# A two-layer diffusion block and an MoE block on one core: the first projection starts with half of its tokens

## The chip, the cores and the metric
One core of one Trainium2 chip runs the whole computation in one launch. The metric is the device time in microseconds; the value of a kernel is the median of its runs. A separate profiled execution gives the trace.

## What is computed
A first block of two layers, then a second block, all in float32, on 256 latent tokens x and 256 context tokens ctx of width 1024. Only the start of the first layer matters here:

```python
silu_c, silu_cc = silu(c), silu(c_ctx)
shift, scale, gate       = split(silu_c  @ w_ada[0] + b_ada[0], 3)   # for the latents
shift_c, scale_c, gate_c = split(silu_cc @ w_ada[0] + b_ada[0], 3)   # for the context
u  = h  * (1.0 + scale)   + shift        # h  = x
uc = hc * (1.0 + scale_c) + shift_c      # hc = ctx
q, k, v, g     = split(u  @ a_w_in)      # 1024 -> 2560 columns
qc, kc, vc, gc = split(uc @ a_w_in)
```

Rotary embedding, windowed attention, an output projection and a normalisation follow, then a layer with neighbourhood attention, then the second block: attention beside a convolution, and a mixture of 32 experts.

## The kernel before, in words
**Tokens.** Activations are kept with features on the 128 partitions: tile j of `H` and `uT` holds features 128j to 128j+127 of all 512 tokens, columns 0 to 255 the latents, 256 to 511 the context. The inputs come token by token, so TensorE turns them: `turn_rows(half)` (L718) does two 128x128 transposes for each of eight tiles into PSUM banks 1 to 4 and waits from the fifth tile on for VectorE, which copies each tile of 256 columns into `H` (L1614 to L1617). Half 0 is x, half 1 ctx. `turn_taps` (L709) turns the convolution's weights for a much later stage.

**Weights.** Big weights are loaded in chunks of 1024x512 (2 MB) into a ring of six slots. `PLAN` (L111) fixes their order: ada0 column chunk 0, ada0 chunk 2, the first a_w_in chunk, ada0 chunks 1 and 3, the second a_w_in chunk, and so on. (This text counts ada0's chunks in the order of their use, from 0.) SyncE issues them in the loop at L553; x is issued after the first chunk and ctx after the second (L567), and from the seventh on SyncE waits until the slot's last reader on TensorE is done (L564). Each chunk has one semaphore count, `full[slot]`, on which `landed(n)` (L700) waits. The small vectors and the taps are issued by ScalarE at the start (L1324 to L1327).

**Modulation.** `stream("ada0", c, bank)` (L729) multiplies chunk c with the SiLU of the two conditioning vectors, in 64 small matmul instructions. ScalarE copies the row out of PSUM (L1340), `fold` (L747) turns it into columns, and VectorE's `take_half(half, bank)` (L1651) makes the scales and shifts of feature tiles 0 to 3 or 4 to 7: two additions and one more for 1 + scale. `modulate` (L1644) then makes `uT` tile by tile, x and ctx in turn, one step of `u_ok` per tile. Chunks 0 and 1 give what tiles 0 to 3 need, chunks 2 and 3 what tiles 4 to 7 need.

**First projection.** Its first chunk has four jobs of 128 output columns, one per PSUM bank. Each is the sum over eight feature tiles, and `half_job(i, ks)` (L835) does four of these with all 512 tokens. The order on TensorE is written out by hand: chunk 0, turn x, chunk 1, fold, turn ctx, turn taps, fold; wait for the taps and the chunk; lower halves of jobs 0 and 1, chunk 2, lower half of job 2, chunk 3, fold, lower half of job 3, fold; then the upper halves, each followed by a rotation for the rotary embedding (`beside`, L807). A float32 product counts as two instructions in the profile, a transpose as one. Behind that, `seven_products` (L858) does other chunks in seven products of half the size for eight.

Of the kernel before, what the change touches and what calls it, by code (L numbers as in the profile page):

```python
# [21 lines left out]
P = 128  # L22
D = 1024
KT = D // P
S = 256
# [202 lines left out]
def build(nc, IN, consts_dram, relpad, out):  # L228
    CA, CN = const_layout()
    with ExitStack() as ctx:  # L230
# [141 lines left out]
        cst_in, vec_in, sink_in = sem("cst_in"), sem("vec_in"), sem("sink_in")  # L372
# [4 lines left out]
        pe_x, x_ok = sem("pe_x"), sem("x_ok")  # L377
        sil_ok = sem("sil_ok")
# [157 lines left out]
        def _(sp):  # L536
# [16 lines left out]
            for n, (stage, src, l, c) in enumerate(PLAN):  # L553
                if n - SLOTS == PLACE["b_in"][5]:
                    sp.wait_ge(st["b_in"], used["b_in"][5])
                    load_bias(range(4))
                    sp.dma_start(late_tables, consts_dram[:, CA["dist"][0]:CA["mult"][1]]).then_inc(table_in, 16)
                if n == PLACE["ada1"][2]:
                    sp.wait_ge(tk["a_in", "dve"], len(DVE_ORDER["a_in"]))
                if n - SLOTS == PLACE["mod_a"][0]:  # L560
                    load_bias(range(4, NH))
                if n >= SLOTS:
                    was = PLAN[n - SLOTS][0]
                    sp.wait_ge(st[was], used[was][PLACE[was].index(n - SLOTS)])  # L564
                w = IN[src][l, :, c * COLS:(c + 1) * COLS].rearrange("(k p) n -> p k n", p=P)
                sp.dma_start(slot(n), w).then_inc(full[n % SLOTS], 16)
                if n in (0, 1):  # L567
                    rows = IN[("x", "ctx")[n]][0].rearrange("(t p) f -> p t f", p=P)
                    sp.dma_start(xrows[:, 2 * n:2 * n + 2, :], rows).then_inc(x_in[n], 16)
                if n == 5:  # L570
                    sp.dma_start(flat[:, 0:CN - CR], consts_dram[:, CR:CN]).then_inc(table_in, 16)
                    for c0, c1 in ((CF, CA["dist"][0]), (CA["mult"][1], CR)):
                        sp.dma_start(cst[:, c0:c1], consts_dram[:, c0:c1]).then_inc(table_in, 16)
# [123 lines left out]
        def _(pe):  # L697
# [11 lines left out]
            def turn_taps():  # L709

                pe.wait_ge(taps_in, 16)
                pe.wait_ge(vec_ok, 1)
                for c in range(4):
                    last = tr(ps[:, 0, 256 + 32 * c:256 + 32 * c + CONV_W], crows[:, c * P:(c + 1) * P],
                              ident[0:CONV_W, 0:CONV_W])
                last.then_inc(pe_vec, 1)

            def turn_rows(half):  # L718

                pe.wait_ge(x_in[half], 16)  # L720
                for j in range(KT):
                    i = half * KT + j
                    if i >= 4:
                        pe.wait_ge(x_ok, i - 3)
                    for t in range(2):
                        last = tr(ps[:, 1 + j % 4, t * P:(t + 1) * P], xrows[:, 2 * half + t, j * P:(j + 1) * P], ident)
                    last.then_inc(pe_x, 1)
# [37 lines left out]
            turn_rows(0)  # L765
            stream("ada0", 1, 6)
            fold("ada0", 0, 0, 2, 7)
            turn_rows(1)
            turn_taps()
            fold("ada0", 1, 0, 2, 7)  # L770
# [31 lines left out]
            def src_ready(stage, k):  # L802
                if stage == "a_in":
                    return u_ok, k + 1
# [30 lines left out]
            def half_job(i, ks):  # L835

                for k in ks:
                    if i == 0:
                        pe.wait_ge(u_ok, k + 1)
                    last = mm(ps[:, i, :], slot(PLACE["a_in"][0])[:, k, i * P:(i + 1) * P], uT[:, k, :],  # L840
                              start=(k == 0), stop=(k == KT - 1))
                if k == KT - 1:
                    last.then_inc(st["a_in"], 1)

            pe.wait_ge(taps_ok, 1)
            landed(PLACE["a_in"][0])
            half_job(0, range(4))
            half_job(1, range(4))
            stream("ada0", 2, 5)
            half_job(2, range(4))  # L850
            stream("ada0", 3, 6)
            fold("ada0", 2, 0, 2, 4)
            half_job(3, range(4))
            fold("ada0", 3, 0, 2, 4)
            for i in range(4):
                half_job(i, range(4, KT))
# [458 lines left out]
        def _(act):  # L1315
# [11 lines left out]
            act.dma_start(sink[:, :], IN["a_sink"].broadcast_to([P, NH])).then_inc(sink_in, 16)  # L1327
# [262 lines left out]
        def _(dve):  # L1590
# [23 lines left out]
            for i in range(2 * KT):  # L1614
                half, j = i // KT, i % KT
                dve.wait_ge(pe_x, i + 1)
                v.tensor_copy(H[:, j, half * S:(half + 1) * S], ps[:, 1 + j % 4, 0:S]).then_inc(x_ok, 1)  # L1617
            dve.wait_ge(pe_vec, 2)
            v.tensor_copy(conv_taps[:, :, :],
                          ps[:, 0, 256:384].rearrange("p (c k) -> p c k", c=4)[:, :, 0:CONV_W]).then_inc(taps_ok, 1)  # L1620
# [44 lines left out]
            dve.wait_ge(x_ok, 2 * KT)  # L1665
            settle()
            modulate(0, range(4))
            take_half(1, 4).then_inc(mod_ok, 1)
            dve.wait_ge(mod_ok, 1)
            modulate(0, range(4, KT))  # L1670
# [92 lines left out]
            dve.wait_ge(u_ok, KT)  # L1763
# [143 lines left out]
            dve.wait_ge(sink_in, 16)  # L1907
# [99 lines left out]
            dve.wait_ge(u_ok, 2 * KT)  # L2007
# [378 lines left out]
```

## Time and profile before

| what | us |
|---|---|
| median of 3 runs | 1213.71 |
| lowest and highest run | 1211.02, 1214.12 |
| the profiled execution | 1209.34 |
| its span in the trace | 1207.3 |
| TensorE busy (PE) | 1152.9 |
| VectorE busy (DVE) | 544.6 |
| ScalarE busy (ACT) | 295.7 |

The times of a trace are counted from the start of its span. The profiled execution's own time is 2.04 us longer than the span. PE is TensorE's matmuls, PEld its weight loads, which overlap them; SPq is SyncE's sequencer issuing transfers. An engine's idle time matters only where something on the way to the end waits for it. Matmuls are pipelined, so the duration of one is longer than its distance to the next.

### The profile page before, as it was taken

The page shows a single profiled execution, that of the slowest core. Times are in us where ns is not written, and L with a number is a line of the kernel's source. Part 1 is how long each engine was busy: PE and PEld are TensorE (multiplying, and loading weights), DVE is VectorE, ACT ScalarE, POOL GpSimd, SP SyncE. Part 2 cuts the span into 40 slices and gives each one's busy share as a digit, 9 for nine tenths or more (in the row PEclk, how much of TensorE's full clock was granted, in tenths as well). Part 3 has the DMA queues.
Part 4 walks back from the last instruction along what each step waited for, and adds up shares of the span by engine and source line. Part 5 has one row for each costly group of instructions (what it writes and reads, how often), then busy time and mean ns, then how long its engine had stood idle before and what let it go on. Part 6 is the DMA issues. An engine that isn't in the chain of part 4 may idle for free.

```text
span 1207.3 us, 17553 instructions
## 1 busy us (share of the span) xinstructions
PE 1152.9 (95%) x7148; PEld 743.0 (62%) x7148; DVE 544.6 (45%) x1278; ACT 295.7 (24%) x705; POOL 22.7 (2%) x33
## 2 busy tenths in 40 slices
PE   4999999989999999999998998999999999999996
PEld 3486876668778888668885585444444444444442
DVE  3353339986575430872799623122222222222223
ACT  0000128850340001660612413111111111111112
POOL 0000000000000001110000000000000000000000
PEclk9999999999999999999999798999999999999999
DMA  9852128023442226566376695999999999999990
GB/s 344 318 209 73 68 93 326 1 75 136 140 178 101 70 70 183 124 188 211 140 279 228 246 301 202 428 427 428 426 429 428 427 429 429 427 428 430 427 413 39
DMA packets 82335, 311.54 MB, mean 258 GB/s; under 512 B 18130, under 2 KB 19229, under 8 KB 69467
## 3 DMA queue, kind: packets, MB, share of 16 engines
q1 hardware_dynamic: 78672, 309.56, 65.9%
q10 hardware_dynamic: 3386, 0.86, 0.3%
q8 instruction: 48, 0.79, 0.3%
q0 software_dynamic: 208, 0.17, 0.1%
q14 instruction: 21, 0.16, 0.0%
HBM read 309.40 MB, written 1.18 MB: 257 GB/s over the span
## 4 chain that ended last, share of the span: by engine, by line
PE 81%; DVE 12%; ACT 2%; DMA 2%; issue 1%; SPq 1%; ACTq 0%; DVEq 0%
PE ps L1246 18%; PE ps L891 17%; PE ps L1278 9%; PE ps L1212 5%; PE ps L992 5%; PE ps L1224 5%; DVE G L2146 4%; PE ps L956 2%; PE ps L942 2%; PE ps L840 2%; PE ps L1096 2%; PE ps L1072 2%; PE ps L929 2%; PE ps L743 2%; DMA ring<-in_a_w_in 2%; DVE soft L1824 1%
## 5 line engine op out<-in xcount | busy, mean ns | idle before, releaser
L1246 PE MATMUL ps<-ring,prob 128*64 128x512 f32 x704 | 188.1, 593 | 1.2 <-issue 1.2
L1246 PEld LDWEIGHTS ps<-ring,prob 128*64 128x64 f32 x704 | 61.9, 137 | 100.3 <-issue 100.3
L2311 DVE TENSOR_TENSOR prob<-ps,prob 128x512 f32<-128x512 f32 x16 | 17.2, 1075 | 193.7 <-PE ps L1246 193.7
L1278 PE MATMUL ps<-ring,prob 128*64 128x512 f32 x352 | 78.0, 596 | 0.0
L891 PE MATMUL ps<-U,ring 128*128 128x256 f32 x304 | 69.9, 381 | 1.6 <-DVE Q L1991 1.3
L1246 PE MATMUL ps<-K,prob 128*64 128x512 f32 x160 | 70.3, 592 | 0.0
L1212 PEld LDWEIGHTS ps<-bias,U 128*128 128x128 f32 x512 | 60.5, 198 | 13.4 <-issue 13.4
L1387 ACT ACTIVATE prob<-ps,soft 128x512 f32<-128x512 f32 (+2 forms) x112 | 64.1, 591 | 11.0 <-DVE soft L1829 9.0
L2319 DVE TENSOR_TENSOR probT<-ps,cst 128x512 f32<-128x512 f32 x32 | 22.1, 691 | 94.6 <-PE ps L1278 94.6
L1212 PE MATMUL ps<-bias,U 128*128 128x128 f32 x512 | 63.5, 284 | 1.1 <-DVE bias L2272 1.1
L891 PEld LDWEIGHTS ps<-U,ring 128*128 128x128 f32 x304 | 57.6, 190 | 9.9 <-DVE Q L1991 1.7
L1224 PE MATMUL ps<-probT,bias 128*128 128x512 f32 x128 | 57.9, 594 | 0.0
L1551 ACT ACTIVATE prob<-ps 128x512 f32<-128x512 f32 x16 | 9.6, 597 | 192.4 <-PE ps L1246 192.4
L1404 ACT ACTIVATE probT<-ps 128x512 f32<-128x512 f32 (+1 forms) x88 | 48.2, 585 | 34.4 <-PE ps L942 33.6
L992 PE MATMUL ps<-U,ring 128*128 128x256 f32 x256 | 56.4, 381 | 0.0
L1544 ACT ACTIVATE prob<-ps,H 128x128 f32<-128x128 f32 x64 | 24.0, 456 | 128.3 <-PE ps L1212 128.3
L942 PE MATMUL ps<-cst,prob 128*128 128x128 f32 x344 | 51.6, 288 | 2.4 <-DVE prob L1850 2.4
L992 PEld LDWEIGHTS ps<-U,ring 128*128 128x128 f32 x256 | 48.4, 190 | 7.1 <-issue 0.8
L1278 PEld LDWEIGHTS ps<-ring,prob 128*64 128x64 f32 x352 | 24.3, 137 | 45.8 <-issue 45.8
L929 PE MATMUL ps<-K,Q 64*128 64x512 f32 (+1 forms) x192 | 46.9, 568 | 1.9 <-ACT G L1375 1.3
L2296 DVE TENSOR_TENSOR U<-ps,U 128x512 f32<-128x512 f32 x64 | 44.2, 691 | 8.9 <-PE ps L1224 8.9
L2146 DVE SCALAR_TENSOR_TENSOR G<-G,conv_taps 128x256 f32<-128x256 f32 x120 | 47.7, 478 | 0.0
(378 smaller groups left out, 1839.2 us busy)
## 6 DMA issues: line engine op xcount, KB each, us to landing
ring<-in_w_exp_gate SPq DMA_DIRECT2D x22, 2048.0 KB, 18.2
ring<-in_w_exp_up SPq DMA_DIRECT2D x20, 2048.0 KB, 16.7
ring<-in_w_exp_down SPq DMA_DIRECT2D x20, 2048.0 KB, 19.9
ring<-in_w_ada SPq DMA_DIRECT2D x12, 2048.0 KB, 16.4
ring<-in_w_mod SPq DMA_DIRECT2D x12, 2048.0 KB, 8.8
ring<-in_b_w_in SPq DMA_DIRECT2D x8, 2048.0 KB, 9.0
ring<-in_a_w_in SPq DMA_DIRECT2D x5, 2048.0 KB, 17.7
ring<-in_w_in SPq DMA_DIRECT2D x5, 2048.0 KB, 9.2
```

The source lines that it names most:

```text
L891: last = mm(ps[:, bank, 0:256], still[:, k, f * P:(f + 1) * P], moving[:, k, :], start=(k == 0), stop=(k == 3))
L929: last = mm(ps[:, 2 * (n % 2) + x, 0:len(kts) * P], q_of(h, kind, qb), k_of(h, kts), start=True, stop=True)
L942: last = tr(ps[:, 4 + i // 2, (i % 2) * S + x * P:(i % 2) * S + (x + 1) * P], prob[:, n % AHEAD, x * T + i * P:x * T + (i + 1) * P], ident)
L992: last = mm(ps[:, m % 4, 0:width], slot(n)[:, k, (m % 4) * P:(m % 4 + 1) * P], src[:, k, 0:width], start=(k == 0), stop=(k == KT - 1))
L1212: last = mm(ps[:, j // 4, (j % 4) * P:(j % 4 + 1) * P], h2rows[:, t, j * P:(j + 1) * P], pick[:, t, :], start=(t == 0), stop=(t == 1))
L1224: mm(ps[:, ACC_BANK[i], :], wpickT[:, t * P:(t + 1) * P], yrows[:, c * 512:(c + 1) * 512], start=True, stop=True).then_inc(scat, 1)
L1246: last = mm(ps[x * CAP:(x + 1) * CAP, 2 + i, :], xg[:, k, x * CAP:(x + 1) * CAP], chunk(n, 2 * i + x, turn)[0][:, k, :], start=(k == 0), s ...
L1278: last = mm(ps[x * CAP:(x + 1) * CAP, 5 + c, :], hidT[:, k, x * CAP:(x + 1) * CAP], chunk(n, 4 + x, turn)[0][:, k, c * 512:(c + 1) * 512], ...
L1387: last = a(prob[:, n % AHEAD, x * T:x * T + w], ps[:, 2 * (n % 2) + x, 0:w], ACT.Exp, bias=s[:, 1, x:x + 1], accum_out=None if L == "c" el ...
L1404: a(probT[:, i * S:i * S + w], ps[:, 4 + i // 2, 0:w], ACT.Copy).then_inc(at["copied"], 1)
L2146: ins = v.scalar_tensor_tensor(convo[:, j, :], glu[:, j, k:k + S], conv_taps[:, j, k:k + 1], convo[:, j, :], ALU.mult, ALU.add)
L2296: v.tensor_tensor(y, ps[:, b, :], y, ALU.add).then_inc(acc_ok, 1)
```

## The change
The loads: ada0's chunk 1 goes ahead of x; the first a_w_in chunk is split by feature tiles, the lower half (tiles 0 to 3) issued after x and ahead of ctx, the upper half after ada0's chunk 3. The lower half has a semaphore of its own, `lower_in`. The sink's load counts on the taps' semaphore, whose waits go to 32.

On TensorE: chunk 1 right behind chunk 0; four tiles of x turned into banks 1 to 4 of their own, both folds, the other four tiles in pairs (a pair fills a bank); the taps. Then the lower halves run on 256 columns at a time: jobs 0 and 1 on x, half of ctx turned, jobs 2 and 3 on x, the rest of ctx turned, and the same jobs on ctx with chunks 2 and 3 between them. The upper halves run on all 512 tokens, as before. VectorE copies pairs of tiles in one instruction (`take_rows`) and makes the first four tiles of u for x, then those for ctx. `u_ok` counts four more.

```diff
@@ -369,12 +369,13 @@
 
 
         table_in = sem("table_in")
-        cst_in, vec_in, sink_in = sem("cst_in"), sem("vec_in"), sem("sink_in")
+        cst_in, vec_in = sem("cst_in"), sem("vec_in")
         x_in, taps_in, taps_ok = [sem("x_in"), sem("ctx_in")], sem("taps_in"), sem("taps_ok")
         rel_in, rel_out, rel_zero = sem("rel_in"), sem("rel_out"), sem("rel_zero")
         full = [sem(f"full{i}") for i in range(SLOTS + 3)]
         pe_vec, vec_ok = sem("pe_vec"), sem("vec_ok")
         pe_x, x_ok = sem("pe_x"), sem("x_ok")
+        lower_in = sem("lower_in")
         sil_ok = sem("sil_ok")
         st = {n: sem(n + "_done") for n in ("ada0", "a_in", "a_out", "ada1", "b_in", "b_out", "mod_a", "c_in",
                                             "c_out", "mod_b")}
@@ -563,10 +564,17 @@
                     was = PLAN[n - SLOTS][0]
                     sp.wait_ge(st[was], used[was][PLACE[was].index(n - SLOTS)])
                 w = IN[src][l, :, c * COLS:(c + 1) * COLS].rearrange("(k p) n -> p k n", p=P)
-                sp.dma_start(slot(n), w).then_inc(full[n % SLOTS], 16)
-                if n in (0, 1):
-                    rows = IN[("x", "ctx")[n]][0].rearrange("(t p) f -> p t f", p=P)
-                    sp.dma_start(xrows[:, 2 * n:2 * n + 2, :], rows).then_inc(x_in[n], 16)
+                if n == PLACE["a_in"][0]:
+                    first_w = w
+                    sp.dma_start(slot(n)[:, 0:4, :], w[:, 0:4, :]).then_inc(lower_in, 16)
+                else:
+                    sp.dma_start(slot(n), w).then_inc(full[n % SLOTS], 16)
+                if n in (1, 2):
+                    rows = IN[("x", "ctx")[n - 1]][0].rearrange("(t p) f -> p t f", p=P)
+                    sp.dma_start(xrows[:, 2 * n - 2:2 * n, :], rows).then_inc(x_in[n - 1], 16)
+                if n == 4:
+                    first = PLACE["a_in"][0]
+                    sp.dma_start(slot(first)[:, 4:KT, :], first_w[:, 4:KT, :]).then_inc(full[first % SLOTS], 16)
                 if n == 5:
                     sp.dma_start(flat[:, 0:CN - CR], consts_dram[:, CR:CN]).then_inc(table_in, 16)
                     for c0, c1 in ((CF, CA["dist"][0]), (CA["mult"][1], CR)):
@@ -708,23 +716,20 @@
 
             def turn_taps():
 
-                pe.wait_ge(taps_in, 16)
-                pe.wait_ge(vec_ok, 1)
+                pe.wait_ge(taps_in, 32)
+                pe.wait_ge(x_ok, 4)
                 for c in range(4):
-                    last = tr(ps[:, 0, 256 + 32 * c:256 + 32 * c + CONV_W], crows[:, c * P:(c + 1) * P],
+                    last = tr(ps[:, 4, 256 + 32 * c:256 + 32 * c + CONV_W], crows[:, c * P:(c + 1) * P],
                               ident[0:CONV_W, 0:CONV_W])
                 last.then_inc(pe_vec, 1)
 
-            def turn_rows(half):
-
-                pe.wait_ge(x_in[half], 16)
-                for j in range(KT):
-                    i = half * KT + j
-                    if i >= 4:
-                        pe.wait_ge(x_ok, i - 3)
+            def turn_rows(half, js, bank):
+
+                for i, j in enumerate(js):
                     for t in range(2):
-                        last = tr(ps[:, 1 + j % 4, t * P:(t + 1) * P], xrows[:, 2 * half + t, j * P:(j + 1) * P], ident)
-                    last.then_inc(pe_x, 1)
+                        last = tr(ps[:, bank, i * S + t * P:i * S + (t + 1) * P],
+                                  xrows[:, 2 * half + t, j * P:(j + 1) * P], ident)
+                last.then_inc(pe_x, 1)
 
             def stream(stage, c, bank):
 
@@ -762,12 +767,15 @@
                 fold(stage, chunks[-1], v0, nv, to)
             pe.wait_ge(sil_ok, 1)
             stream("ada0", 0, 5)
-            turn_rows(0)
             stream("ada0", 1, 6)
+            pe.wait_ge(x_in[0], 16)
+            for j in range(4):
+                turn_rows(0, (j,), 1 + j)
             fold("ada0", 0, 0, 2, 7)
-            turn_rows(1)
+            fold("ada0", 1, 0, 2, 7)
+            turn_rows(0, (4, 5), 5)
+            turn_rows(0, (6, 7), 6)
             turn_taps()
-            fold("ada0", 1, 0, 2, 7)
 
             def in_proj(stage, src, widths, after=None, skip=0):
                 jobs = JOBS[stage]
@@ -801,7 +809,7 @@
 
             def src_ready(stage, k):
                 if stage == "a_in":
-                    return u_ok, k + 1
+                    return u_ok, 4 + k + 1
                 return nm["rms1", "out"], k + 1
 
             def beside(i):
@@ -832,28 +840,48 @@
                 mm(ps[:, 4 + n % 2, 0:S], rotm, src, start=True, stop=True).then_inc(rot_done, 1)
 
 
-            def half_job(i, ks):
-
-                for k in ks:
+            def lower_job(i, c0):
+
+                for k in range(4):
                     if i == 0:
-                        pe.wait_ge(u_ok, k + 1)
+                        pe.wait_ge(u_ok, (k + 1 if c0 == 0 else 4 + k + 1))
+                    mm(ps[:, i, c0:c0 + S], slot(PLACE["a_in"][0])[:, k, i * P:(i + 1) * P], uT[:, k, c0:c0 + S],
+                       start=(k == 0 and c0 == 0), stop=False)
+
+            def upper_job(i):
+
+                for k in range(4, KT):
+                    if i == 0:
+                        pe.wait_ge(u_ok, 4 + k + 1)
                     last = mm(ps[:, i, :], slot(PLACE["a_in"][0])[:, k, i * P:(i + 1) * P], uT[:, k, :],
-                              start=(k == 0), stop=(k == KT - 1))
-                if k == KT - 1:
-                    last.then_inc(st["a_in"], 1)
-
+                              start=False, stop=(k == KT - 1))
+                last.then_inc(st["a_in"], 1)
+
+            pe.wait_ge(lower_in, 16)
+            lower_job(0, 0)
+            lower_job(1, 0)
+            pe.wait_ge(x_in[1], 16)
+            turn_rows(1, (0, 1), 7)
             pe.wait_ge(taps_ok, 1)
+            turn_rows(1, (2, 3), 4)
+            lower_job(2, 0)
+            lower_job(3, 0)
+            pe.wait_ge(x_ok, 7)
+            turn_rows(1, (4, 5), 7)
+            pe.wait_ge(x_ok, 8)
+            turn_rows(1, (6, 7), 4)
+            lower_job(0, S)
+            stream("ada0", 2, 5)
+            lower_job(1, S)
+            stream("ada0", 3, 6)
+            lower_job(2, S)
+            pe.wait_ge(x_ok, 10)
+            fold("ada0", 2, 0, 2, 4)
+            fold("ada0", 3, 0, 2, 4)
+            lower_job(3, S)
             landed(PLACE["a_in"][0])
-            half_job(0, range(4))
-            half_job(1, range(4))
-            stream("ada0", 2, 5)
-            half_job(2, range(4))
-            stream("ada0", 3, 6)
-            fold("ada0", 2, 0, 2, 4)
-            half_job(3, range(4))
-            fold("ada0", 3, 0, 2, 4)
             for i in range(4):
-                half_job(i, range(4, KT))
+                upper_job(i)
                 beside(i)
             def seven_products(stage, u, beside_product=None):
 
@@ -1324,7 +1352,7 @@
                 act.dma_start(vrows[r:r + n, t, :], flat.rearrange("(r f) -> r f", f=P)).then_inc(vec_in, 16)
                 row += n
             act.dma_start(crows, IN["conv_w_2"][0]).then_inc(taps_in, 16)
-            act.dma_start(sink[:, :], IN["a_sink"].broadcast_to([P, NH])).then_inc(sink_in, 16)
+            act.dma_start(sink[:, :], IN["a_sink"].broadcast_to([P, NH])).then_inc(taps_in, 16)
 
             act.wait_ge(cst_in, 16)
             act.wait_ge(vec_ok, 1)
@@ -1611,13 +1639,15 @@
             dve.wait_ge(cst_in, 16)
             dve.wait_ge(pe_vec, 1)
             v.tensor_copy(vec[:, :], ps[:, 0, 0:NVEC]).then_inc(vec_ok, 1)
-            for i in range(2 * KT):
-                half, j = i // KT, i % KT
-                dve.wait_ge(pe_x, i + 1)
-                v.tensor_copy(H[:, j, half * S:(half + 1) * S], ps[:, 1 + j % 4, 0:S]).then_inc(x_ok, 1)
-            dve.wait_ge(pe_vec, 2)
-            v.tensor_copy(conv_taps[:, :, :],
-                          ps[:, 0, 256:384].rearrange("p (c k) -> p c k", c=4)[:, :, 0:CONV_W]).then_inc(taps_ok, 1)
+            for j in range(4):
+                dve.wait_ge(pe_x, j + 1)
+                v.tensor_copy(H[:, j, 0:S], ps[:, 1 + j, 0:S]).then_inc(x_ok, 1)
+
+            def take_rows(half, j, bank, count):
+
+                dve.wait_ge(pe_x, count)
+                v.tensor_copy(H[:, j:j + 2, half * S:(half + 1) * S],
+                              ps[:, bank, :].rearrange("p (i t) -> p i t", i=2)).then_inc(x_ok, 1)
 
             def take_modulation(l):
                 stage = f"ada{l}"
@@ -1662,11 +1692,27 @@
 
             dve.wait_ge(vec_ok, 1)
             step(take_half(0, 7))
-            dve.wait_ge(x_ok, 2 * KT)
+            dve.wait_ge(x_ok, 4)
             settle()
-            modulate(0, range(4))
+            for j in range(4):
+                v.tensor_scalar(uT[:, j, 0:S], H[:, j, 0:S], mod[:, 0, 8 + j, 0:1], mod[:, 0, j, 0:1],
+                                ALU.mult, ALU.add).then_inc(u_ok, 1)
+            take_rows(0, 4, 5, 5)
+            take_rows(0, 6, 6, 6)
+            dve.wait_ge(pe_vec, 2)
+            v.tensor_copy(conv_taps[:, :, :],
+                          ps[:, 4, 256:384].rearrange("p (c k) -> p c k", c=4)[:, :, 0:CONV_W]).then_inc(taps_ok, 1)
+            take_rows(1, 0, 7, 7)
+            take_rows(1, 2, 4, 8)
+            dve.wait_ge(x_ok, 8)
+            for j in range(4):
+                v.tensor_scalar(uT[:, j, S:T], H[:, j, S:T], mod[:, 0, 8 + j, 1:2], mod[:, 0, j, 1:2],
+                                ALU.mult, ALU.add).then_inc(u_ok, 1)
+            take_rows(1, 4, 7, 9)
+            take_rows(1, 6, 4, 10)
             take_half(1, 4).then_inc(mod_ok, 1)
             dve.wait_ge(mod_ok, 1)
+            dve.wait_ge(x_ok, 10)
             modulate(0, range(4, KT))
...
```

## Rows read from the trace of the kernel before

**Rows 1.** page, busy time by engine, and granted clock in 40 slices
```profile
PE 1152.9 (95%) x7148; PEld 743.0 (62%) x7148; DVE 544.6 (45%) x1278; ACT 295.7 (24%) x705; POOL 22.7 (2%) x33
...
PEclk9999999999999999999999798999999999999999
```

**Rows 2.** chain of waits, 0 to 130 us: start us, us, what
```profile
8.61 20.25 DMA ring<-in_a_w_in
...
28.95 7.11 PE ps L840 x16
...
48.73 7.13 PE ps L840 x16
...
64.03 3.45 PE ps L891 x16
```

**Rows 3.** windows: busy us (and count) by engine, PEclk, DMA share, GB/s
```profile
26.84:28.95 2.11, 0.01 (x2) 0.04 (x1) 1.97 (x10) 0.00 (x0) 0.00 (x0) 1.00 1.05 387
28.95:47.44 18.49, 18.48 (x164) 9.79 (x164) 1.37 (x5) 0.56 (x2) 0.00 (x0) 1.00 1.05 386
47.44:48.73 1.29, 0.00 (x0) 0.00 (x0) 1.20 (x6) 0.00 (x0) 0.00 (x0) 1.00 1.04 384
```

**Rows 4.** timeline of PE, 15 to 29 us: start us, us, what
```profile
15.16 3.64 PE L743 MATMUL ps<-ring,sil 128*32 128x128 f32 x64 [2.11 <-ACT sil L1332]
18.73 3.01 PE L726 MATMUL ps<-cst,Q 128*128 128x128 f32 x16
21.67 1.95 PE L743 MATMUL ps<-ring,sil 128*32 128x128 f32 x64
23.55 0.39 PE L753 MATMUL ps<-cst,prob 128*128 128x8 f32 x2
23.80 2.36 PE L726 MATMUL ps<-cst,Q 128*128 128x128 f32 x16
```

**Rows 5.** weight loads, grouped, 18.73 to 20.8 and 20.9 to 21.67 us
```profile
L726 PEld LDWEIGHTS ps<-cst,Q 128*128 128x128 f32 x11 | 2.2, 226 | 0.4 <-issue 0.4
...
L726 PEld LDWEIGHTS ps<-cst,Q 128*128 128x128 f32 x6 | 0.8, 157 | 0.0
```

**Rows 6.** timeline of SyncE's queue: issue us, us, what
```profile
1.64 0.58 SPq L569 DMA_DIRECT2D Q<-in_x  x1
2.27 0.47 SPq L566 DMA_DIRECT2D ring<-in_w_ada  x1
2.78 5.79 SPq L569 DMA_DIRECT2D Q<-in_ctx  x1
```

**Rows 7.** DMA issues, short stretches at 1.6 to 3: KB, us to landing
```profile
Q<-in_x SPq DMA_DIRECT2D x1, 1024.0 KB, 11.1
...
ring<-in_w_ada SPq DMA_DIRECT2D x1, 2048.0 KB, 18.6
Q<-in_ctx SPq DMA_DIRECT2D x1, 1024.0 KB, 20.7
```

**Rows 8.** timeline of DVE, 19 to 28 us
```profile
19.46 3.08 DVE L1617 COPY H<-ps 128x256 f32<-128x256 f32 x8 [5.95 <-PE ps L726]
...
27.11 0.23 DVE L1655 TENSOR_TENSOR mod<-ps,vec 128x8 f32<-128x8 f32 x2
...
27.65 0.41 DVE L1646 TENSOR_SCALAR U<-H,mod 128x256 f32<-128x256 f32 x1
```

**Rows 9.** waits of SyncE's queue: us in total, times, longest
```profile
SPq L583 <- PE ps L1246: 181.9, 28, 22.6
...
SPq L566 <- PE ps L840: 20.3, 1, 20.3
```

**Rows 10.** chain of waits, start of the expert stage
```profile
733.25 5.93 PE ps L1212 x32
...
754.72 3.77 PE ps L1212 x32
```

More of the change, by code:

```diff
@@ L1761, in add_up @@
                                     ).then_inc(hsum_ok, 1)
-            dve.wait_ge(u_ok, KT)
+            dve.wait_ge(u_ok, 4 + KT)
             token_sums("a_in", "t2")
@@ L1905, in bias_c @@
                 settle()
-            dve.wait_ge(sink_in, 16)
+            dve.wait_ge(taps_in, 32)
             step(v.tensor_scalar(negsink[:, :], sink[:, :], -1.0, None, ALU.mult))
@@ L2006, in _ @@
                 take_q(m)
-            dve.wait_ge(u_ok, 2 * KT)
+            dve.wait_ge(u_ok, 4 + 2 * KT)
             dve.wait_ge(col_done, CHUNKS["ada1"] + 6)
```

## The prediction

> **What bounds the kernel now.** I began with the page. TensorE is busy for 1152.9 of 1207.3 us, and its granted clock stands near full in all but two of forty slices [rows 1]. So a microsecond is won where TensorE is idle or slow. The profiled execution took 1209.34 us, 2.04 more than its span; the median of the three runs, 1213.71, is 4.37 higher, and they spread over 3.1. I make the sum against the profiled execution and take its difference off the median.
>
> Next I read the chain of waits over the first 130 us [rows 2]. Until 28.86 its last link is a transfer: TensorE's first product with the first a_w_in chunk starts at 28.95, when that chunk has landed. The upper half of the four jobs starts at 48.73.
>
> The table by stretches shows two holes [rows 3]. From 26.84 to 28.95 TensorE does nothing for 2.11 us while the 16 DMA engines are full: the weights are not in. From 47.44 to 48.73 it does nothing for 1.29: VectorE turns the folded columns of ada0's chunks 2 and 3 into scales and makes tile 4 of u. Together 3.40 us. Between them 18.49 us of work stand solid: the lower half of four 512-column jobs (16 products, 32 instructions), two modulation chunks, two folds.
>
> Last I read TensorE's start by instruction [rows 4]. The same 64 small matmuls take 3.64 us for chunk 0 and 1.95 for chunk 1: TensorE begins at 1.2 GHz and has gone to 2.4 in between. The weight loads of the transposes put the rise near 20.9 us: 226 ns each until 20.8, 157 after 20.9 [rows 5]. The windows view prints 1.00 for all of its stretches there; the durations tell more.
>
> **The transfers, reordered.** All big loads go through SyncE's queue [rows 6]. Issue plus time to landing [rows 7] gives x 12.7, ada0 chunk 1 20.9, ctx 23.5; a_w_in chunk 0 landed at 28.9 [rows 2]. From 20.9 on, 1 MB costs 2.6 to 2.7 us and 2 MB 5.4. Chunk 1 took 8.2 behind x, 2.8 more than that.
>
> The new order behind chunk 0 is chunk 1 (2 MB), x (1), lower a_w_in (1), ctx (1), chunks 2 and 3 (2 each), upper a_w_in (1), a_w_in chunk 1. Counted in bytes, x now ends where chunk 1 did: 20.9. Then lower a_w_in 23.5, ctx 26.2, chunk 2 31.6, chunk 3 37.0, the upper half 39.7, a_w_in chunk 1 45.1, as before. Chunk 1 lands between 18.2 (20.9 less x's 2.7) and, if nothing had been lost by then, 15.4.
>
> One transfer becomes two, so SyncE issues one more. The row of ctx bounds the cost: a 1 MB transfer lands 2.6 us after the 2 MB one ahead of it, just its share of bytes. I add nothing. The Trainium skill's page "DMA: Bandwidth & Descriptors" (sections on the anatomy of one DMA and the rules for authors) fits a fixed 2.0 us to each DMA and advises joining small ones. Were that paid in line, ctx would land at 28.2 and the upper half near 41.7, both still ahead of use below; the sum would stand, with ctx's cover gone.
>
> **TensorE's new order.** Prices: a chunk 1.88 (21.67 to 23.55), a fold 0.25 (23.55 to 23.80), a transpose 0.147 (2.36 for sixteen) [rows 4]; the taps' four 0.44, which is what is left of 23.55 to 26.84 (3.29) after sixteen transposes and two folds. Four products of 256 columns cost 1.73: the first seven-product unit has eight in 3.45 [rows 2]. Four of 512 cost 3.45, the pair of jobs at 28.95 being 7.11 for twice that. So halving the columns costs nothing and all lower halves are 13.8 us on either side, the doubled weight loads covered as they are in that row.
> - Chunk 0 runs 15.16 to 18.73, as before. Chunk 1 now follows it, where x's transposes stood, and has landed. At 0.056 us each, 39 of its 64 are done by 20.9; the rest take 0.73: 21.65. It costs 2.92 instead of 1.88.
> - Eight transposes of x (in since 20.9), 22.8; folds 0 and 1, 23.3; eight transposes, 24.5; taps, 24.95. Their wait now takes in the sink's load, on the same semaphore, issued at 7 us: no cost.
> - VectorE copies the first four tiles at 0.385 (3.08 for eight), done near 23.4; take_half starts at 23.6 and takes 0.54 (27.11 to 27.65); the first tile of u is there at 24.6 and another after each 0.41 at most [rows 8]. TensorE takes one per 0.43 from 24.95.
> - Lower jobs 0 and 1 on x, 28.4. Lower a_w_in was in at 23.5, ctx at 26.2. VectorE has by then made u's four tiles (25.8), the two pairs (at most 0.77 each) and the taps. Eight transposes of ctx, 29.6; jobs 2 and 3 on x, 33.05; eight more, 34.2. Each pair is copied behind the next job.
> - Job 0 on ctx 35.95, chunk 2 37.8 (in since 31.6), job 1 39.55, chunk 3 41.4 (in since 37.0), job 2 43.15, folds 43.65, job 3 45.4.
> - VectorE starts at 43.7 on take_half (0.54) and tile 4 (two of 0.41): 45.1. The last job hides it, by 0.3; uncovered, it would be the hole of 1.29 again, and tile 4 is what is late next.
>
> That is 45.4. Before, the changes between kinds of work cost 0.43: 18.49 less 13.8, two chunks (3.76) and two folds (0.5). I put 0.4 in again, as half of the changes are the same and those between transposes and products are new; bounds 0 and 1.0. The upper half starts at **45.8, 2.9 us earlier**. Check from the other side: 15.16 to 26.84 was 11.68; the same work is now 3.57 + 2.92 + 32 x 0.147 + 0.5 + 0.44 = 12.13, so 0.45 goes to the low clock, and 3.40 - 0.45 = 2.95.
>
> **Does it pass through?** The upper jobs, the rotations and seven-product units follow in unchanged order. a_w_in chunk 1 is in at 45.1 and was first multiplied at 64.03, now 61.1 [rows 2]. After that SyncE waits for TensorE, not the reverse: 20.3 us for the end of the upper jobs, 181.9 in the expert stage [rows 9]. So all moves together: 1209.34 - 2.9 = 1206.4 for a profiled execution, 1213.71 - 2.9 = 1210.8 for the median. That is 0.24%; a measurement of this kernel can tell about 0.3% from no change.
>
> **Rivals.**
> *The low clock later falls elsewhere (0.17).* In slices 23 and 24 the clock dips [rows 1], and the first group of 32 in the expert stage takes 5.93 us against 3.77 for the next [rows 10]: 2.16 us that hang on where the low clock lies. Moved by 3 us, the work may miss it, or meet it with as much more: gain 5.1 or 0.7, 1208.6 or 1213.0. For it: such dips exist. Against: the lull before keeps its length.
> *x comes late and TensorE stays at 1.2 GHz (0.09): the slower side.* The first product now hangs on x, which is put behind 2 MB; before it landed 6 us ahead of use. If chunk 1 comes after 18.73 or x after 21.65, TensorE idles where it was busy when the clock rose. If x takes ctx's old landing, 23.5, that is a wait of 1.9; if TensorE also stays at 1.2 GHz to 28, about half of the 7 us from 20.9, 3.5, is lost: 5.4 - 2.9 = 2.5 slower, 1216.2. It decides the sign from a loss of 2.9, with x later than 24.5 if the clock is left out. Against: the byte count, and that behind the holes of 2.11 and 1.29 us the same products ran at the full rate [rows 2, 3]. [...]
> *The gain is given back (0.12).* VectorE gets a new stretch ahead of ctx; if tile 4 of u comes late, the second hole (1.29) returns, and the changes of work may cost 0.6 more: gain 1.0, 1212.7. For it: tile 4 has only 0.3 of cover. Against: the other steps have 1 us or more.
>
> **How the numbers follow.** The forecast has 0.62. Its own bounds are gains of 2.3 (changes at 1.0) and 3.4 (at nothing), 1210.3 to 1211.4, and medians of such runs scatter by over a microsecond more. Of it 0.21 lies beyond a gain of 3.6 us, of the clock rival 0.09: faster 0.30. Slower by over 0.3%: 0.06, from the late x. The rest, 0.64, is within. The range, 1207.6 to 1213.6, takes in the clock rival and the returned hole and leaves out the late x and the edges of scatter.
>
> **What would show it.** Right: x in near 21 and lower a_w_in near 23.5; first product near 24.95 with no hole ahead; the lower halves in 13.8 us; the upper half from 45.8; each later piece of the chain 2.9 earlier to the end. Wrong: TensorE waiting for Q<-in_x; 64 small matmuls at 3.6 us twice; a hole before tile 4; a lead lost at a lull of TensorE, near 220, 605 or 733 us.

## The result and the profile after

The changed kernel's median is 1202.49 us (4 runs, 1201.32 to 1202.62) beside 1212.74 of the kernel before (a fourth run, 1211.77, stands beside the three of the table above): ratio 0.9921, 95% interval [0.9908, 0.9933]. A ratio, here and below, is an estimate over all runs of both kernels and differs a little from the quotient of the two medians. It is 0.8% faster, about 10 us, where 2.9 us were forecast. Its profiled execution took 1202.58 us with a span of 1200.6, 6.7 below the 1207.3 of before [rows 1]. So even the two profiles differ by more than the forecast, and the medians by 3.5 us more than the profiles.

The chain of waits of the changed kernel, 0 to 60 us (start us, us, what), answers to [rows 2]:

```profile
2.26 18.59 DMA Q<-in_x
...
20.89 0.45 PE ps L730 x2
...
23.25 0.42 DVE U L1698
...
23.81 3.69 PE ps L848 x16
27.50 0.87 PE ps L730 x8
28.37 3.46 PE ps L848 x16
...
44.22 6.87 PE ps L856 x16
...
59.25 3.45 PE ps L919 x16
```

The transfer at the head is now x, landed at 20.85. The first product stands at 23.81 (28.95 before), the upper half at 44.22 (48.73), the first seven-product unit at 59.25 (64.03). Both holes are gone. The transfers came as counted in bytes: lower a_w_in landed at 23.45 (forecast 23.5) and ctx at 26.07 (26.2), so the one more transfer cost nothing that shows. The timeline of PE, 14 to 24 us, answers to [rows 4]:

```profile
14.17 3.20 PE L748 MATMUL ps<-ring,sil 128*32 128x128 f32 x64 [2.11 <-ACT sil L1360]
18.29 1.95 PE L748 MATMUL ps<-ring,sil 128*32 128x128 f32 x64 [0.92 <-DMA ring<-in_w_ada]
20.89 1.09 PE L730 MATMUL ps<-cst,Q 128*128 128x128 f32 x8 [0.65 <-DMA Q<-in_x]
```

TensorE waits three times now, 0.92 us for chunk 1, 0.65 for x and, right before its first product, 0.19 for u. Chunk 1 takes 1.95 us, what it took at 2.4 GHz before, so the clock is up from its start, which the forecast did not have. The table by stretches (busy us by engine, PEclk, DMA share, GB/s) answers to [rows 3]:

```profile
23.81:44.22 20.41, 20.41 (x213) 17.71 (x214) 7.89 (x22) 0.55 (x2) 0.00 (x0) 1.00 1.05 387
```

From the first product to the upper half TensorE is busy without a gap for 20.41 us, at a granted clock of 1.00.

**Where the rest of the 6.7 us lies.** The lead of the changed kernel, piece by piece of the two chains: 4.51 us at the upper half, 4.78 at the first seven-product unit, 4.75 at the modulation chunks near 485 us (485.69 against 480.94), 4.99 at TensorE's last group (1192.85 against 1187.86), 7.5 where VectorE goes on behind the expert loop, 6.7 at the end. In between it swings with stretches of low clock. The chain behind the last matmul, before:

```profile
1197.54 3.08 issue
...
1200.84 1.21 DVE U L2351 x2
1202.05 0.09 DVE soft L2353
...
1202.15 0.75 DVE Q L2357
```

and in the changed kernel:

```profile
1192.56 0.53 issue
...
1193.32 1.20 DVE U L2397 x2
...
1194.61 0.81 issue
1195.42 0.75 DVE Q L2403
```

"Issue" is time in which VectorE waited for nothing that the profile shows. It is 3.08 us in one piece before and 0.53 and 0.81 after, 1.7 less, on lines that the diff doesn't touch.

### The profile page after: what moved, and what is told of

Its sections match the earlier page's. It is cut to its first block, busy times and chain, and to the rows that moved or that the text cites. A ratio compares the mean times of both kernels' runs of the same rounds, so it can differ in the third digit from the quotient of the medians.

```text
span 1200.6 us, 17614 instructions
## 1 busy us (share of the span) xinstructions
PE 1151.1 (96%) x7180; PEld 747.7 (62%) x7180; DVE 545.0 (45%) x1272; ACT 295.8 (25%) x705; POOL 22.9 (2%) x33
## 4 chain that ended last, share of the span: by engine, by line
PE 83%; DVE 12%; ACT 2%; DMA 2%; issue 1%; SPq 0%; DVEq 0%; ACTq 0%
PE ps L1274 18%; PE ps L919 17%; PE ps L1306 9%; PE ps L1240 5%; PE ps L1020 5%; PE ps L1252 5%; DVE G L2192 4%; PE ps L984 2%; PE ps L970 2%; PE ps L1124 2%; PE ps L1100 2%; PE ps L957 2%; PE ps L748 2%; DMA Q<-in_x 2%; DVE soft L1870 1%; DVE prob L1896 1%
## 6 DMA issues: line engine op xcount, KB each, us to landing
ring<-in_w_exp_up SPq DMA_DIRECT2D x20, 2048.0 KB, 16.6
ring<-in_w_exp_down SPq DMA_DIRECT2D x20, 2048.0 KB, 20.8
```

## The experiments

The experiments ran in four groups, each with runs of the kernel before (medians 1210.9 to 1212.0). A ratio is against the ones of the same group. The changed kernel itself ran again in the first group only (e2); later groups are compared with it through their ratios.

**Both kernels once more.** No edit.

> The kernel before, unchanged, once more. Theory A (the gain is made in the opening): its first product with a_w_in starts near 28.95 us again, its upper half near 48.7, and all its runs lie within 1211 to 1214 us. Theory B (half of the gain is luck of the later stages): the pieces that differed between the two profiles behind 64 us move between these two runs of one program as well: the 3.08 us of 'issue' at the exit of the expert loop (0.53 in the changed kernel), the 5.93 us of the first expert group, and the 1.2 us lost near 541 us; its profile then lies 2 to 4 us off the first one's 1207.3.

> The changed kernel, unchanged, once more, on the same chip as e1. Theory A: 10 us below e1 in the median, upper half near 44.2 us. Theory B: the profile again gains 4.5 us up to the upper half and the rest of the 10 us comes and goes; the ratio moves towards 0.995. If the low clock of TensorE ends near 21 us here and not near 17, the first product stands near 24.9 us instead of 23.8.

Measured: 1212.98 us (ratio 1.0004 [0.9992, 1.0015]) and 1203.06 (0.9923 [0.9908, 0.9938]). The result stands. e2's profile repeats the first one (span 1201.2, upper half at 44.47). e1's doesn't: its span is 1211.0, 3.7 above the first profile of the same program. From its chain:

```profile
28.91 0.09 issue
29.00 8.80 PE ps L840 x16
...
50.48 7.13 PE ps L840 x16
```

The first pair of lower jobs takes 8.80 us instead of 7.11 [rows 2], and the upper half starts 1.75 later. The windows view says why:

```profile
26.60:28.95 2.35, 0.06 (x1) 0.00 (x0) 2.21 (x10) 0.00 (x0) 0.00 (x0) 1.00 1.06 390
28.95:33.00 4.05, 4.00 (x6) 1.73 (x7) 1.18 (x4) 0.00 (x0) 0.00 (x0) 0.58 1.05 386
33.00:40.00 7.00, 7.00 (x77) 3.80 (x76) 0.00 (x0) 0.25 (x1) 0.00 (x0) 1.00 1.05 386
```

Behind the first hole the granted clock is 0.58 of full speed: mostly 1.2 GHz. The first profile of the kernel before was one in which this did not happen. Its hole was also the shorter one: TensorE sat idle for 2.10 us ahead of the first product there, for 2.34 in e1. A second difference is a stop in the middle of TensorE's modulation chunks near 490 us, where nothing is waited for: 1.27 us in e1, 0.66 in the first profile, none in either profile of the changed kernel. The lines of e1 and of the changed kernel (timelines of PE):

```profile
492.28 0.42 PE L743 MATMUL ps<-ring,sil 128*32 128x128 f32 x7 [1.27 <-issue]
```

```profile
480.94 3.70 PE L748 MATMUL ps<-ring,sil 128*32 128x128 f32 x128
```

**The loads alone.**

```diff
-            turn_rows(0)
             stream("ada0", 1, 6)
+            turn_rows(0)
...
-            landed(PLACE["a_in"][0])
+            pe.wait_ge(lower_in, 16)
```

with SyncE's loop as in the changed kernel.

> Kernel before with the new order of loads and chunk 1 multiplied ahead of the turning of x, but all lower jobs on 512 tokens. Theory A: the first product waits for ctx (landed 26.2), its eight transposed tiles and the scales behind them: 30.3 us instead of 28.95; the second hole of 1.3 us stays; about 1.3 us slower than the kernel before (+0.5 to +2). Rival (the earlier lower weights are what pays): first product at 23.5 to 26, several us faster than before.

Measured: 1214.49 us, ratio 1.0026 [1.0015, 1.0036]: slower by 0.26%. The chain goes ctx, its eight copies, the first tile of u; the first product stands at 31.81, 1.5 later than forecast, since VectorE, not TensorE, paces the copies and take_half waits for the last of them. The clock fell here too: TensorE waited 2.90 us for ctx, the granted clock between 26.60 and 28.95 was 0.50, and the first pair of jobs took 8.80 us instead of 7.11. So e3 pays the 1.7 us of clock that e1 pays too, and its loss is the later start: the upper half stands at 53.38, 2.9 us behind e1's 50.48. The new order of loads is worth less than nothing unless jobs can start without ctx.

**TensorE's order alone.** The changed kernel with x behind chunk 0 and ctx behind chunk 1, as before the change; the weights still in halves.

> Changed kernel with the old order of loads: x, ada0 chunk 1, ctx, lower a_w_in, upper a_w_in. Theory A: the lower weights land at 26.2 us, the first product stands there and everything behind it keeps its length, 20.4 us: upper half at 46.6, 2.4 us slower than the changed kernel and 2.1 faster than before in the opening. Rival (only the new order of TensorE's work counts, loads are ahead anyway): no difference from the changed kernel.

Measured: 1207.92 us, ratio 0.996 [0.9945, 0.9975]; 4.9 us slower than the changed kernel, 3.9 faster than before (medians of one group). The first product stands at 27.30, 1.1 later than forecast. Not the weights hold it but chunk 1, landed at 21.0 and taking 3.42 us (chain of waits):

```profile
2.27 18.73 DMA ring<-in_w_ada
...
21.04 3.42 PE ps L748 x64
24.46 0.38 PE ps L730 x2
...
27.30 3.69 PE ps L848 x16
```

TensorE idled 2.43 us before it, and the 64 matmuls took 3.42 us instead of 1.95: it was mostly at 1.2 GHz. The upper half starts at 47.71, 3.2 us behind e2's 44.47, and this is what the order of loads is worth once the work is in the new order. Against the first profile's 48.73 the order of work alone wins only 1.0 us of opening. The rest of e4's 3.9 us is not opening: it too has no low clock behind the first product, no stop near 490 us and VectorE's short end.

**The second hole.**

```diff
-            fold("ada0", 2, 0, 2, 4)
-            fold("ada0", 3, 0, 2, 4)
             lower_job(3, S)
+            fold("ada0", 2, 0, 2, 4)
+            fold("ada0", 3, 0, 2, 4)
```

> Changed kernel with folds 2 and 3 behind the last lower job instead of ahead of it. Theory A (the second hole is what those folds' new place closes): TensorE idles about 1.3 us ahead of the upper half, which starts at about 45.6 instead of 44.3; 1.3 us slower than the changed kernel, ratio to before near 0.9935. Rival (it was covered anyway): no difference.

Measured: 1204.51 us, ratio 0.994 [0.9926, 0.9953]. That is 0.0017 or some 2 us above e2's ratio, and the intervals overlap; the place is plain. From first product to upper half it takes 21.71 us instead of 20.41, 1.3 more, and the hole is back in its chain, from the folds' end at 44.26 to 45.64:

```profile
43.90 0.36 PE ps L758 x4
...
44.76 0.41 DVE U L1676
...
45.64 7.11 PE ps L856 x16
```

**VectorE's end.** Five memsets of one column each at VectorE's start.

```diff
+            for i in range(5):
+                v.memset(mod2[:, i:i + 1], 0.0)
             v.memset(sil[:, :, :], 0.0).then_inc(sil_zero, 1)
```

> Changed kernel with five tiny memsets more at VectorE's very start, where it idles; so VectorE's program up to the expert loop is as long as before the change (1631 instructions in the trace against 1626). Theory P (the end is shorter because VectorE's shorter program lies otherwise in its fetched blocks): the wait behind the loop goes from 0.53 and 0.9 back to about 2.8 us, 1.4 us slower than the changed kernel, all of it behind the last matmul. Rival (those waits are TensorE's lead or chance): they stay at 0.53 and 0.9 and the time stays.

Measured: 1203.64 us, ratio 0.9936 [0.9923, 0.995]. The median moves by less than the intervals can tell, but the place is plain. Behind the loop stand, in its chain,

```profile
1191.29 2.78 issue
...
1194.30 1.20 DVE U L2399 x2
...
1195.61 0.75 DVE Q L2405
```

one wait of 2.78 us and no long one later, as before the change. The total of the waits goes from 1.34 to 2.78, so 1.4 us. Every profile of the changed kernel and of e4, e5, e8 and e11 to e13 ends the short way, every one of the kernel before and its variants the long way. Five instructions of no use at the start of VectorE's program bring it back. That it is the fetching of VectorE's program was my reason for trying it; no run shows that. What they show is that these five instructions, at a place where VectorE idles, decide; length and layout of the program can't be told apart.

**The first hole, filled.** 14 transposes of the identity into a bank in which nothing is needed.

```diff
+            for _ in range(14):
+                tr(ps[:, 5, 0:P], ident, ident)
             pe.wait_ge(taps_ok, 1)
             landed(PLACE["a_in"][0])
```

> Kernel before with 14 transposes of the identity into a free bank while it waits for the first a_w_in chunk, 2.1 us of work in the first hole. Theory C (the hole costs more than its length, because the clock granted after it is sometimes 1.2 GHz for 3.4 us, as in the second run of the kernel before): no low clock between 25 and 40 us, first product still at 28.9, upper half at 48.7 in each profile; 0.5 to 1.7 us faster than before in the median. Rival (the hole costs its 2.1 us and no more): same median as before. TensorE's longer program may also move its own fetch wait near 490 us (0.9).

Measured: 1209.38 us, ratio 0.9984 [0.9975, 0.9993]; no low clock in the opening, upper half at 48.79. The transposes end 0.77 us ahead of the first product, so part of the hole stays. But the stop near 490 us was gone too, so two causes were mixed. The next run took TensorE's program length alone, with 32 transposes at its very start:

> Kernel before with 32 transposes of the identity at TensorE's very start, where it waits for the small vectors (from 2.6 us on). TensorE's program is then about as much longer as the change makes it; nothing of the order is touched. Theory P (TensorE waits 0.9 us near 490 us in the kernel before because a block of its program comes late there, and not in the changed one): that wait is gone and the stretch from attention b to attention c takes 165.6 instead of 167.2 us; 1.0 to 1.5 us faster than before. Rival (in the kernel with the filled hole it was the filling that paid): no difference here, the stretch at 167.2. The first hole and its possible low clock stay in both.

Measured: 1210.79 us, 0.9992 [0.998, 1.0004]. The stop near 490 is gone here as well, with the low clock still there: the first pair again took 8.80 us. The last pair of runs holds the program length fixed and moves only the place of the 14 transposes.

> Kernel before with 14 transposes of the identity in the first hole, once more. Theory C (the hole lowers the clock in most runs): the granted clock stays at 2.4 GHz through the lower halves, from first product to upper half 19.8 us, about 1 to 1.7 us faster than e15. Rival (the hole costs its length only): same median as e15.

> Kernel before with the same 14 transposes at TensorE's start, hole left open; program lengths as in e14. Theory C: low clock for 3.4 us shortly behind the hole in the profile, 21.5 us from first product to upper half, 1 to 1.7 us slower than e14 in the median. Rival: equal to e14.

Measured: 1209.97 and 1212.10 us, 11 runs each; the means differ by 1.8 us, plus or minus 1.3. The windows view of e15 (hole open), then of e14 (hole filled):

```profile
26.60:28.95 2.35, 0.00 (x0) 0.02 (x1) 2.21 (x10) 0.00 (x0) 0.00 (x0) 0.72 1.06 390
28.95:33.00 4.05, 4.04 (x5) 1.83 (x6) 1.10 (x4) 0.00 (x0) 0.00 (x0) 0.50 1.05 388
33.00:40.00 7.00, 7.00 (x60) 3.45 (x62) 0.00 (x0) 0.00 (x0) 0.00 (x0) 0.89 1.05 386
```

```profile
26.60:28.95 2.35, 1.56 (x15) 1.35 (x14) 2.21 (x10) 0.00 (x0) 0.00 (x0) 1.00 1.05 388
28.95:33.00 4.05, 4.05 (x10) 1.90 (x11) 1.11 (x4) 0.00 (x0) 0.00 (x0) 1.00 1.05 385
```

In e15 the first pair took 9.84 us and the upper half began at 51.49; in e14 7.11 and 48.73. Of the five profiles of a kernel with the old opening and the hole open (the first, e1, e9, e10, e15), four show the low clock behind it; of the two with the hole filled, none. The first one, on which the whole prediction rests, is the odd one. It also has the shortest hole: TensorE's idle time before the first product is 2.10 us in it and 2.34, 2.41, 2.55 and 2.39 in e1, e9, e10 and e15, for instance in e10 (timeline of PE):

```profile
28.40 2.48 PE L840 MATMUL ps<-U,ring 128*128 128x512 f32 x3 [2.55 <-DMA ring<-in_a_w_in]
```

Whether those tenths or chance spared the first profile is not shown; no run moved the hole's length alone.

**The straggling part of each load.** The taps are 31 rows of 2 KB in one load.

```diff
-            act.dma_start(crows, IN["conv_w_2"][0]).then_inc(taps_in, 16)
+            for r0, r1 in ((0, 16), (16, 24), (24, 28), (28, 30), (30, 31)):
+                act.dma_start(crows[r0:r1], IN["conv_w_2"][0, r0:r1]).then_inc(taps_in, 16)
```

> Changed kernel with the taps' load of 31 rows (62 KB) cut into loads of 16, 8, 4, 2 and 1 rows. Theory D (the last of the sixteen parts of each big load comes 1.6 to 2 us behind the others because one DMA engine has all 31 rows): x lands near 19.2 us instead of 20.9, lower a_w_in near 22, first product at 22.2 to 22.8 instead of 23.8; 1 to 1.6 us faster than the changed kernel. Rival (the lag comes from the sink's or the bias tables' small pieces): x at 20.9, no difference.

> Kernel before with the taps' load cut into 16, 8, 4, 2 and 1 rows. Theory D: the first a_w_in chunk lands near 27.4 us instead of 28.9 (as lower parts landed 1.4 to 2 earlier in the changed kernel with this cut), the first hole shrinks by as much, 1.3 to 1.9 us faster than before. Rival: TensorE or VectorE holds the first product back to 28.9 by itself: no difference.

Measured: with the changed kernel 1202.60 us, 0.9922 [0.9909, 0.9936], the same as without; with the kernel before 1209.11, 0.9981 [0.997, 0.9992]. The load of x took, from issue, 16.6 us in e8 and 18.8 in e2:

```profile
Q<-in_x SPq DMA_DIRECT2D x1, 1024.0 KB, 16.6
```

```profile
Q<-in_x SPq DMA_DIRECT2D x1, 1024.0 KB, 18.8
```

So one load of 62 KB held back a megabyte by 2.2 us; the sink's load was the same in both, so the rival is out. It doesn't help the changed kernel much, since chunk 1 was then still running: 64 + 64 small matmuls from 14.51 to 20.6, the first half of them at the low clock (6.07 us for all, where a chunk takes 1.95 at the high one), first product at 23.42. In the kernel before, a_w_in lands 0.6 earlier (28.31), under half of the 1.5 expected, and its stop near 490 us happens to be gone too; how the 2.7 us divide was not tried.

**TensorE at the high clock from the start.** 50 transposes of the identity ahead of the small vectors, with the taps' cut and without; then 64 and 20 more up to chunk 0, with the cut.

> Changed kernel with the taps' cut and 50 transposes of the identity from 2.6 us to about 12, so TensorE is at 2.4 GHz when chunk 0 comes. Theory E (with x in at 18.8 the opening is held by TensorE's low clock): chunk 0 takes 1.9 us instead of 3.2, chunk 1 runs from 16.7 to 18.7, first product at 21.5 to 22, upper half near 42.3: 1.5 to 2 us faster than the changed kernel with the cut alone. Rival (the next load, lower a_w_in near 21.5, or VectorE's chain holds it): below 0.7.

> Changed kernel with the same 50 transposes but the taps in one load. Theory: x lands at 20.9 and holds the first product, so the high clock alone gains nothing, first product at 23.7 as before (0 to 0.3 us). Rival (the low clock is what the changed kernel's opening pays): 1 us or more faster.

> Changed kernel with the taps' cut, 64 transposes of the identity ahead of the small vectors and 20 more behind them, up to chunk 0. Theory E (TensorE's low clock holds the opening once x is in at 18.8): clock high from about 7 us on, chunk 0 in 1.9 us instead of 3.2, chunk 1 from 16.8 to 18.7, first product at 21.5 to 22 (lower a_w_in lands near 21.5 to 22.8), 1 to 2 us faster than the changed kernel with the cut alone, 1200.5 to 1201.5 us. Rival: the first product is held by the lower weights or by VectorE's chain, 0 to 0.7.

Measured: 1202.14 (0.9917 [0.9902, 0.9931]), 1202.60 (0.9926 [0.9913, 0.994]) and 1200.69 (0.9916 [0.9901, 0.993]). The first two tested nothing: the transposes ended at about 10 us, and the windows view of e12 shows the clock down again when chunk 0 came:

```profile
10.00:14.00 4.00, 0.53 (x2) 0.28 (x2) 0.35 (x1) 1.51 (x2) 0.96 (x2) 0.78 0.98 343
14.00:17.50 3.50, 3.50 (x64) 2.96 (x64) 0.00 (x0) 0.00 (x0) 0.00 (x0) 0.50 1.05 403
```

In e13 each chunk ran in 1.95 us. But then TensorE waited 0.48 us for chunk 1, 0.57 for x and 0.40 for the lower weights:

```profile
22.88 3.72 PE L852 MATMUL ps<-U,ring 128*128 128x256 f32 x16 [0.40 <-DMA ring<-in_a_w_in]
```

The first product stands at 22.88, 0.9 us ahead of the changed kernel and 0.5 ahead of e8, not 2. The rival was right, the loads hold the opening. The median is the lowest of all, but the six runs lie in two lots, four at 1200.1 to 1200.8 and two at 1204.9, and the ratio can't be told from the changed kernel's; no version here beats it clearly.

## Why the prediction was wrong

**The mechanism was right.** x landed at 20.85 (forecast 20.9), the first lower half was reached without ctx, the second hole closed, nothing in the opening stood in the way of the upper half. Lower halves of 256 columns cost next to nothing more: 14.55 us in all against 14.28 before, where both had been put at 13.8. TensorE's wait for x, named as a sign of being wrong, did appear (0.65 us), but only because TensorE was there early. SyncE waits for TensorE later, and the lead of the opening was kept.

**The opening's term was too small by 1.6 us.** The upper half came 4.51 us earlier, not 2.9. Of this 1.14 is the first product, 23.81 instead of 24.95. I took the rise of the clock from the one profile, 20.9 us, as a fixed time, and charged 1.04 to chunk 1 for it; here chunk 1 ran at full speed. The small vectors came sooner as well (chunk 0 from 14.17, not 15.16; over all profiles that start varies). So TensorE was ready before x and began to turn it at 20.89, not 21.65: 0.76. From there to the first product took 2.92 us, not 3.30: the price of a transpose, 0.147, was read where VectorE's copies paced them, and eight take 0.87 here, 0.109 each. The rest is the 0.4 for changes of work: 20.41 us from the first product against 20.85. The products did take 0.7 more than the 13.8 of the sum, but the cheaper transposes and folds had paid for it.

**The step that failed is "Against: ... behind the holes of 2.11 and 1.29 us the same products ran at the full rate".** I took one profiled execution as proof that the clock stays up behind a hole, and used it only against a loss from the change. I never asked what the hole of the kernel before costs in its other executions: it was put at its length, 2.1 us, and the clock behind it at nothing. Four of five profiles with that hole open show the clock at 1.2 GHz behind it, 1.7 to 2.7 us in the first pair of jobs (e1, e9, e10, e15), and e14 against e15 prices it at 1.8 (0.5 to 3.1) in the runs. The changed kernel removes the wait, and with it this price. With its own 2.39 us the hole cost 5.1 us in e15. The Trainium skill's "TensorE: Matmul & The Clock Gate" (section on oscillation) tells of the clock falling again when TensorE waits for a DMA between bursts of matmuls, in a kernel whose waits are longer than these. The traces agree in kind, and show it behind waits of 2.34 to 2.90 us (e3's with the others), though not behind the one of 2.10. The rival "x comes late and TensorE stays at 1.2 GHz" had the right mechanism in the wrong kernel.

**"So all moves together" held for the work, not for the stops.** The change alters the length of VectorE's and TensorE's programs. The end behind the loop got 1.2 to 1.7 us shorter (from TensorE's last group to the end, 12.74 and 12.94 in the two profiles of the changed kernel, 14.45 and 14.17 in the two of before); e6 undoes it with five instructions. The stop near 490 us, 0.66 to 1.27 in the kernel before, was gone. No step of mine asked what a shorter or longer program does elsewhere.

**The sum.** Opening 4.5, low clock behind the hole about 1.8, stop near 490 us 0.7 to 1.3, VectorE's end 1.5: 8.5 to 9.1 us, where 8.8 (e1's group, 1211.83 less 1203.06) to 10.2 were measured. The terms come from single profiles and e14's pair, so the sum is an account, not a proof. The profiles of e1 and e2 give it from another side: 6.0 us at the upper half (50.48 against 44.47, the clock within it), 1.3 at the stop, 1.2 at the end, 8.5 of 9.8; the other 1.3 lie in between and are not assigned. The base was off too: the execution shown for the kernel before, 1209.34, lay 1.6 to 4.4 us under its medians, which I noted and did not explain. It had a high clock behind the hole.

**The range was drawn about the wrong things.** It covered the changes between kinds of work and the scatter, and one low-clock rival of 2.2 us. The cases that came true were all on one side and add up.

**What stays open.** What the stop near 490 us hangs on: e7, e9 and e14, with a longer TensorE program, don't have it; e10, whose TensorE program is as long as before, doesn't either; e3 does. e15, of the length of e14, lost none there either. So it follows the layout of the programs in some way, but not TensorE's length alone. The stretches of low clock near 340, 670 and 730 us (the dips of [rows 1] are slices 23 and 25, not 23 and 24) change in length and place from profile to profile and were not studied; the one near 340 was missing in e6's, which put its later work 1.4 us ahead.

## What to carry to other kernels

Give TensorE whatever half of its work needs the least data, and order loads by the first product that they allow; here the loads alone lost 0.26%, and the order of work alone gave 1.0 of the 4.5 us of opening. A hole in TensorE's work ahead of a dense stretch can cost more than its length. Here 2.34 to 2.55 us of waiting cost 1.7 to 2.7 us more through the clock behind it, in four of five profiles but not in the one that was read. Look at a second profile of the same program before you price a hole. When an execution shown lies well under the medians, find out what it was spared.

## What the runs showed of the hardware

A small load can hold back a large one beside it: with 31 rows of 2 KB in one load, 62 KB, a 1 MB load took 18.8 us to land (e2), with the same rows cut into 16, 8, 4, 2 and 1 it took 16.6 (e8). The Trainium skill's "DMA: Bandwidth & Descriptors" (section on why a DMA increments its semaphore by 16) says that a transfer is spread over the largest number of engines, at most 16, that divides its number of rows, which for 31 rows is one; the two runs fit that, though no view here shows which engine was late. 14 idle transposes (1.7 us of work) into a free bank kept the granted clock at 1.00 through a wait for weights (e7, e14), worth 1.8 us, plus or minus 1.3. 50 transposes that ended 4 us ahead of the work did nothing for it: the granted clock was 0.50 when it came (e12). And five instructions more at the start of VectorE's program, beside some 1270 that the page counts, moved its end by 1.4 us (e6).
